# A two-block transformer kernel on one core: the gate columns of one projection last, and another order of work where the latent projections begin

## The reference, cut to what matters

```python
# first block: S = 256 rows, D = 2048, three groups of 16 heads of 128 columns
proj = rmsnorm(x, norm_b) @ w_in_b                # 3 * 2048 query columns, 2048 gate columns
q_all, gate = proj[..., :3 * D], proj[..., 3 * D:]
for g in range(3):                                # dilations 1, 4, 16
    q = apply_rope(q_all[:, :, g]); outs[g], lses[g] = dilated_window_attention(q, k, v, ...)
merged = softmax(lses over g)-weighted sum of outs
x = x + (merged * silu(gate)) @ w_out_b
# second block, where its second layer starts: x is the sum after the product with a_w_out
h_kv = rms_norm(x, kv_norm_g) * (1 + kv_scale) + kv_shift;  c_kv, k_r = split(h_kv @ kv_w_dkv)   # 576 columns
h    = rms_norm(x, norm_g[1]) * (1 + scale) + shift;        c_q, z   = split(h @ b_w_in)         # 2560 columns
```

## Time and profile before

| | |
|---|---|
| three runs | 2191.84, 2192.15, 2194.24 us; median 2192.15 |
| profiled execution | 2189.68 us, of it 2188.0 us from the first to the last instruction |
| PE busy | 2110.7 us, 96% |
| DVE, ACT busy | 1574.4 us (72%), 1097.3 us (50%) |
| mean granted clock of PE | 0.986 |
| DMA | 523.34 MB, 239 GB/s on average |

### The profile page before, as it was taken

One profiled execution on the slowest core, in us unless ns is written; L12 is line 12 of the kernel. 1 busy time (PEld: TensorE's weight loads), 2 busy tenths in 40 slices (PEclk: granted clock), 3 DMA queues, 4 the chain that ended last, 5 costly groups with the idle time before them and its releaser, 6 DMA issues.

```text
span 2188.0 us, 29739 instructions
## 1 busy us (share of the span) xinstructions
PE 2110.7 (96%) x9732; PEld 1746.1 (80%) x9732; DVE 1574.4 (72%) x2506; ACT 1097.3 (50%) x1683; POOL 11.6 (1%) x25
## 2 busy tenths in 40 slices
PE   7999999999999999979899999999999979999988
PEld 6888888888887878757788888888888868878867
DVE  5766777787879888857787778778765565556654
ACT  5444554445444444436544445454444365867742
POOL 0000000000000000000000000000000000000000
PEclk9999999999999999979999999999999989999999
DMA  7876678878766666647688777778744536433333
GB/s 294 293 281 252 239 276 320 301 283 289 264 254 235 228 256 227 222 166 259 232 296 297 289 296 298 278 293 285 301 185 173 192 125 240 173 131 139 136 134 134
DMA packets 93395, 523.34 MB, mean 239 GB/s; under 512 B 10337, under 2 KB 10593, under 8 KB 47489
## 3 DMA queue, kind: packets, MB, share of 16 engines
q1 hardware_dynamic: 90736, 509.60, 63.8%
q0 software_dynamic: 2032, 8.46, 1.1%
q10 hardware_dynamic: 544, 4.19, 0.5%
HBM read 518.01 MB, written 4.19 MB: 239 GB/s over the span
## 4 chain that ended last, share of the span: by engine, by line
PE 86%; DVE 5%; ACT 4%; issue 2%; DMA 2%; DVEq 0%; SPq 0%; ACTq 0%
PE bank L441 78%; PE bank L459 2%; DMA raw<-units 2%; DVE w_lo L1426 1%; PE bank L578 1%; ACT w_hi L847 1%; DVE ada_raw L1437 1%; PE bank L682 1%; PE bank L481 0%; PE bank L784 0%; PE bank L782 0%; PE bank L475 0%; PE bank L515 0%; DVE rbuf L1542 0%; PE bank L488 0%
## 5 line engine op out<-in xcount | busy, mean ns | idle before, releaser
L847 ACT ACTIVATE w_hi<-raw 128x1024 fp32r<-128x1024 f32 (+2 forms) x702 | 726.0, 1047 | 899.2 <-PE bank L441 665.8
L1426 DVE TENSOR_TENSOR w_lo<-raw,w_hi 128x1024 fp32r<-128x1024 f32 (+2 forms) x702 | 832.9, 1207 | 409.5 <-ACT w_hi L847 407.1
L441 PE MATMUL bank<-w_hi,xa_hi 128*128 128x512 f32 x1952 | 770.9, 395 | 5.6 <-DVE w_lo L1426 2.8
L441 PE MATMUL bank<-w_hi,xa_lo 128*128 128x512 f32 x1952 | 761.6, 390 | 0.0
L441 PE MATMUL bank<-w_lo,xa_hi 128*128 128x512 f32 x1952 | 761.2, 390 | 0.0
L441 PEld LDWEIGHTS bank<-w_hi,xa_hi 128*128 128x128 f32 x1952 | 367.7, 188 | 82.8 <-issue 6.1
L441 PEld LDWEIGHTS bank<-w_hi,xa_lo 128*128 128x128 f32 x1952 | 367.2, 188 | 77.6
L441 PEld LDWEIGHTS bank<-w_lo,xa_hi 128*128 128x128 f32 x1952 | 367.7, 188 | 74.6
L441 PE MATMUL bank<-w_hi,xb_hi 128*128 128x512 f32 (+2 forms) x864 | 336.9, 390 | 6.6 <-DVE rbuf L1563 3.6
L441 PE MATMUL bank<-w_hi,xb_lo 128*128 128x512 f32 (+2 forms) x864 | 330.2, 382 | 0.0
L441 PE MATMUL bank<-w_lo,xb_hi 128*128 128x512 f32 (+2 forms) x864 | 330.0, 382 | 0.0
(11 more groups left out here) (237 smaller groups left out, 1241.3 us busy)
## 6 DMA issues: line engine op xcount, KB each, us to landing
raw<-units SPq DMA_DIRECT2D x351, 1024.0 KB, 4.8
ada_raw<-ada_units SPq DMA_DIRECT2D x256, 512.0 KB, 5.5
rows<-ln_rows POOLq DMA_DIRECT2D x8, 512.0 KB, 3.8
res<-x SPq DMA_DIRECT2D x4, 512.0 KB, 7.6
held<-res ACTq DMA_DIRECT2D x1, 2048.0 KB, 11.9
rows<-norm_row POOLq DMA_DIRECT2D x2, 1024.0 KB, 6.2
res<-held ACTq DMA_DIRECT2D x1, 2048.0 KB, 7.8
out<-res SPq DMA_DIRECT2D x4, 512.0 KB, 7.5
```

Source lines behind the costliest of these rows:

```text
L441: last = pe.matmul(ps[t][:, 0:cols], l, r, start=c == 0 and k == 0, stop=c == CPU * units_of - 1 and k == 2)
L847: act.activation(half_of(w_hi, n0, i), half_of(raw, n0, i), ACT.Copy).then_inc(hi_done, 1)
L1426: dve.tensor_tensor(half_of(w_lo, n0, i), half_of(raw, n0, i), half_of(w_hi, n0, i), ALU.subtract)\
```

## The change

In stage in_b the order of units is now: four sets of three query blocks (12 units each, `SET_UNITS`), then four gate blocks (16 units, `GATE_UNITS`). The loops over sets are written out. A set's attention stands more densely beside the next set's units (`HEAD_STEPS`), the fourth set's beside the gate blocks; `TAIL_STEPS` is gone. `take_out` writes without the gate into `weighed` (the same storage as `gates`). ACT takes each gate block into `rbuf` (`take_gate`), DVE multiplies (`apply_gate`), and PE, ACT and DVE turn and cut the result (`turn_heads`, `split_heads`) for gate blocks 0 to 2 in the gate steps and for block 3 in out_b. Rope's pieces have new places, and a conversion can have other work between its halves (`hi_half`, `lo_half`). The 32 ada steps that in_b gives up move to out_g, and SP's loads follow.

At the border, ACT squares the first three column blocks during the second half of out_g, and the last one per tile (`add_last_out`). For each group ACT makes the dkv rows alone and copies the transposed rows to `wide` (`turned_rows`); the in_q rows are made from that copy beside dkv's second block (`late_modulated`). The eight dkv loads fetch only the 288 columns used. `turn_ahead` transposes one group a step, here and at the start of the kernel. The gains are computed earlier, halfway through out_g.

```diff
-HEAD_STEPS = {2: [("scores", 0)], 5: [("turn", 0), ("scores", 1)], 6: [("weigh", 0)],
-              8: [("turn", 1), ("scores", 2)], 9: [("weigh", 1)], 11: [("turn", 2), ("scores", 3)],
-              12: [("weigh", 2)], 13: [("turn", 3)], 14: [("weigh", 3)]}
-TAIL_STEPS = {1: [("scores", 0)], 3: [("turn", 0), ("scores", 1)], 4: [("weigh", 0)],
-              5: [("turn", 1), ("scores", 2)],
-              6: [("weigh", 1), ("turn", 2), ("scores", 3), ("weigh", 2), ("turn", 3), ("weigh", 3)]}
+HEAD_STEPS = {2: [("scores", 0)], 4: [("turn", 0), ("scores", 1)], 5: [("weigh", 0)],
+              6: [("turn", 1), ("scores", 2)], 7: [("weigh", 1)], 8: [("turn", 2), ("scores", 3)],
+              9: [("weigh", 2)], 10: [("turn", 3)], 11: [("weigh", 3)]}
...
+SET_UNITS, GATE_UNITS = 12, 16
+GATE_BLOCK0 = BLOCK0["in_b"] + 12
...
+ADA0 = {"in_a": 0, "out_a": 4, "kv": 6, "in_b": 10, "out_b": 14, "in_v": 16, "in_uz": 20, "out_g": 28}
+ADA_STEPS = [{0: 1, 1: 1, 2: 1, 3: 1, 5: 1, 7: 1, 8: 1, 11: 1}] + 3 * [{1: 2, 2: 1, 3: 1, 8: 1, 10: 1, 11: 2}] + [{}]
...
-        gates = res
+        weighed = res
...
+            n0, m0 = UNIT0["in_b"] + 4, 8 * ADA0["in_b"] + 2
+            for table in ADA_STEPS:
+                for q in range(SET_UNITS if table else GATE_UNITS):
+                    load_unit(n0)
+                    n0 += 1
+                    for _ in range(table.get(q, 0)):
+                        load_ada(m0)
...
+            while n0 < UNIT0["in_q"]:
+                sp.wait_ge(lo_done, 2 * (n0 - 2) + 2)
+                dst, src = (a.rearrange("p (i n) -> p i n", i=2)[:, :, 0:CPU // 2 * width(n0)] for a in (raw[n0 % 2][:], units[n0]))
+                sp.dma_start(dst, src).then_inc(raw_in[n0 % 2], 16)
+                n0 += 1
             with Loop(sp, (UNITS - n0) // 2) as j:
...
+                g = i + 2
+                if g < 8:
...
+            def turn_heads(b):
+                pe.wait_ge(gated, b + 1)
                 for i in range(2):
...
+            def set_step(j, q):
+                if j and q == 1:
+                    turn_q(2, j - 1)
+                for part, h in HEAD_STEPS.get(q, ()) if j else ():
+                    head_part(part, h, j - 1)
+                if j < 4 and q in (8, 11):
+                    turn_q((q - 8) // 3, j)
+                if j == 4 and q in (5, 9, 13):
+                    turn_heads((q - 5) // 4)
...
+            for j in range(4):
+                for b in range(3):
+                    product("in_b", 3 * j + b, xa, then=lambda q: set_step(j, 4 * b + q),
+                            before=None if j or b else await_rows)
...
+            def await_heads(q):
+                for i in range(2):
+                    g = g0 + 24 + 2 * q + i
+                    pe.wait_ge(turn_free[g % 2], g // 2 + 2)
+            product("out_b", 0, xb, before=await_heads, then=lambda q: turn_heads(3) if q == 0 else None)
...
+            def take_gate(b):
+                act.wait_ge(half_used, 2 * (UNIT0["in_b"] + 4 * SET_UNITS + 4 * b + 4))
+                if b:
+                    act.wait_ge(gated, b)
+                par = (GATE_BLOCK0 + b) % 2
+                for t in range(NT):
+                    act.activation(rbuf[:, t, :], banks[2 * par + t][:], ACT.Silu, scale=stat[:, 4 + t:5 + t])                        .then_inc(bank_free[par], 1)
...
+            for q in range(16):
+                if q == 0:
+                    take_gate(3)
+                elif q == 1:
+                    split_heads(3)
+                    act.wait_ge(gated, 4)
+                    act.dma_start(res[:], held).then_inc(reloaded, 16)
+                elif q == 4:
...
+                    if half == 1 and b:
+                        act.wait_ge(res_ready, 4 + b)
+                        for t in range(NT):
+                            steps.did(act.activation(ubuf[:, t, :], res[:, t, (b - 1) * NB:b * NB], ACT.Square,
+                                                     accum_out=block_sums[:, t, b - 1:b]))
...
+            for g in range(8):
+                at = TURN0["xq"] + g
+                act.wait_ge(turned, at + 1)
+                modulated(turn_bank[at % 2], g, 1, "kvshift", g)
+                act.activation(turned_rows(g), turn_bank[at % 2][:], ACT.Copy).then_inc(turn_free[at % 2], 1)
+                if g in (3, 5):
...
+            junk = [squares[:, t, :] for t in range(NT)]
+            n0 = UNIT0["dkv"] + 4
+            for q in range(4):
+                for i in range(2):
+                    late_modulated(2 * q + i)
+                split_hi(n0 + q)
+                if q == 1:
...
+            def rope_query(j, g, pieces):
+                n = 3 * j + g
+                b0 = BLOCK0["in_b"] + n
+                dve.wait_ge(half_used, 2 * (UNIT0["in_b"] + 4 * n + 4))
+                dve.wait_ge(turned, g0 + 2 * n)
+                rope([banks[2 * (b0 % 2) + t] for t in range(NT)], b0, 0, 0, pieces)
...
+            def apply_gate(b):
+                dve.wait_ge(bank_free[(GATE_BLOCK0 + b) % 2], read_out(GATE_BLOCK0 + b))
+                if b == 3:
+                    dve.wait_ge(small_free[(k0 + 79) % 2], small_read(k0 + 79))
+                for t in range(NT):
+                    last = dve.tensor_tensor(heads_out[:, t, :], weighed[:, t, b * NB:(b + 1) * NB], rbuf[:, t, :], ALU.mult)
+                last.then_inc(gated, 1)
...
+            def set_step(j, q, m):
+                n = UNIT0["in_b"] + SET_UNITS * j + q + 2
+                now, before = (HEAD_STEPS.get(i, ()) if j else () for i in (q, q - 1))
+                for part, h in now:
+                    k = k0 + 20 * (j - 1) + HEAD_USES[part, h]
                     if part == "weigh":
...
+                        take_out(h, k, j - 1)
                     elif part == "scores":
...
+                        mask_scores(k)
+                if j and q == 0:
+                    rope_query(j - 1, 2, ((0, 0), (0, S)))
+                lo_half(n, 0)
+                for part, h in now:
                     if part == "scores":
...
+                        maxima(k0 + 20 * (j - 1) + HEAD_USES[part, h])
+                for part, h in before:
+                    if part == "scores":
+                        add_groups(h, j - 1)
+                lo_half(n, 1)
+                if j and q == 0:
+                    rope_query(j - 1, 2, ((1, 0), (1, S)))
+                if j < 4 and 4 <= q < 8:
+                    rope_query(j, 0, ((q // 2 - 2, q % 2 * S),))
+                if j < 4 and q in (9, 10):
+                    rope_query(j, 1, ((q - 9, 0), (q - 9, S)))
+                if j == 4 and q in (4, 8, 12):
+                    apply_gate(q // 4 - 1)
+                if j == 4 and q in (5, 9, 13):
+                    split_heads((q - 5) // 4)
+                for i in range(ADA_STEPS[j].get(q, 0)):
+                    add_ada(m + i)
+            m0 = 8 * ADA0["in_b"]
+            for j in range(5):
...
+                if q == 1:
+                    split_heads(3)
+                if q != 15:
...
+                if q == 0:
+                    apply_gate(3)
+                if q == 7:
```

More of the change, by code:

```diff
@@ L602, in turn_heads @@
+            def turn_heads(b):
+                pe.wait_ge(gated, b + 1)
                 for i in range(2):
[L603 to L617, removed]
+                    turn(g0 + 24 + 2 * b + i, tiles(heads_out, 2 * P * i))
@@ L623, in _ @@
             for b in range(4):
[L624 to L634, removed]
@@ L637, in _ @@
[L637 to L644, removed]
+                product("in_b", 12 + b, xa, then=lambda q: set_step(4, 4 * b + q))
+            def await_heads(q):
+                for i in range(2):
+                    g = g0 + 24 + 2 * q + i
+                    pe.wait_ge(turn_free[g % 2], g // 2 + 2)
@@ L650, in turn_sum @@
                 turn(TURN0["xg"] + g, tiles(res, 2 * P * g))
-            product("out_b", 2, xb, then=turn_sum)
-            product("out_b", 3, xb, then=lambda q: turn_sum(4 + q) if q < 2 else None)
+            for b in range(1, 4):
+                product("out_b", b, xb, then=lambda q: turn_sum(2 * b - 2 + q) if q < 2 else None)
             for g in (6, 7):
@@ L1084, in _ @@
-            act.wait_ge(spilled, 16)
-            for q in range(16):
-                set_step(q, 0, False)
-                if q == 2:
-                    act.wait_ge(root_row, 1)
-                    act.activation(rows[:], rows[:], ACT.Sqrt, bias=eps).then_inc(root_row, 1)
-            with Loop(act, 3, steps) as j:
-                for q in range(16):
-                    set_step(q, j, True)
-            for q in range(6):
-                if q < 5:
-                    split_hi(UNIT0["out_b"] + q + 2)
-                if q == 0:
-                    copy_q(2, 4, 3)
-                for part, h in TAIL_STEPS.get(q, ()):
+                    copy_turned(g0 + 6 * j + 2 * g + i, side_flat[:, at:at + 2 * S])
@@ L1260, in _ @@
-            for t in range(NT):
```

(26 more changed lines are left out.)

381 lines of the change are left out of this document (182 added, 199 removed).

## The result

The changed kernel takes 2199.55 us (median of 11 runs) against 2192.15 us (11 runs): ratio 1.0035, 95% interval 1.0025 to 1.0045. It is slower by 0.35%, and the forecast was 2199.6. One of its 11 runs took 5494.45 us; the ratio leaves it out, and without it the median is 2199.3. That forecast and median agree to a tenth is partly luck: the price of the clock and the gain at the border were both too small, and they have opposite signs. The profiled execution took 2202.29 us, with a span of 2200.6 against 2188.0.

A forecast was written before the change was run, and what follows sets the result against it. PE was taken as the bound, busy 2110.7 of 2188.0 us; only its waits and clock could change. Terms 9.7 - 3.3 + 1.0 = +7.4 us on the median 2192.15 gave 2199.6 us, range 2184 to 2211.

The forecast's parts named there:

- The bank: In in_b's sets, PE waits before unit 8 for rope's last reader of the shared bank: 3.1 + 3 x 5.2 = +18.7 us.
- Rival B: At unit 8 PE does not wait, as DVE runs far enough ahead: 18.7 and its clock 7.0 fall away, 2173.9; chance 0.13.
- The third block's rope: In the next set, PE's transposes after unit 1 wait 2.5 us for rope, three times: +7.5 us.
- Block 3 of the gate: In out_b, PE's transposes behind unit 0 wait for the gate's product on DVE: +4.8 us.
- Saved in in_b: Gate columns last removes 5.3 us of waits and the tail's 25 us: -30.3 us.
- the tail: The fourth set's attention in out_b costs 25 us beyond its work, which the change removes.
- The clock: Half clock behind the idles before unit 8 and at the gate: 2.0 for each near 5 us, 1.0 for 3.1: +9.0 us.
- The border: Between out_g and in_q: rms 0.65 us earlier, groups' work shorter, DVE pacing the second dkv block: -3.3 us.
- its bound of -6: At the border, the gain if the clock rises one slow stretch earlier: -6 us.
- The forecast's bounds for a narrow load: At the border, a narrow dkv load takes 2.7 to 4.9 us, taken 3.6; at 4.9 the part gives -2.0.
- The start: Group 5's transposes come a step later, delaying unit 2's conversion and unit 4's load: +1.0 us, bounds 0 and +2.5.
- its 9.7: Part 1, gate columns last, in in_b and out_b: -30.3 + 18.7 + 7.5 + 4.8 + 9.0 = +9.7 us.

The follow-up runs named there:

- the first experiment: Changed kernel with the first query block's four rope pieces in steps 4, 5, 5 and 6 instead of 4, 5, 6 and 7: 2172.66 us, 0.9912.
- the old start: Changed kernel with the old order of the transposes in in_a alone, two groups at a time after the first two: 2198.39 us, 1.0025.
- the old border: Changed kernel with squares and root after the output product, both modulations from the turned bank, in_q behind all rows, full-width loads: 2205.74 us, 1.0060.
- the wide loads: Changed kernel with its new border, but the eight narrow units loaded at full width, 1 MB each: 2198.57 us, 1.0030.
- the second experiment: Changed kernel with the third block's rope whole before step 0's conversions, and one ada step of three sets moved from step 11 to 7: 2189.94 us, 0.9988.
- the third: Changed kernel with PE's transposes of the last gate block after out_b's unit 1 instead of unit 0, ACT's and DVE's work a step later: 2193.12 us, 1.0004.
- the two smaller moves: Third block's rope before step 0's conversions and gate block 3 one unit later; with the earlier rope piece, all on the changed kernel: 2158.41 us, 0.9845.

## Why the prediction was right, point by point

**The bank, +18.7: right.** 3.13 us once and 5.05, 5.05 and 5.06 us, 18.3 in sum. The forecast's list gave 5.8 us from unit 7's end to the last reader of the bank less 0.67 for weigh, which is 5.13 and not the 5.2 that it wrote; the chain shows 5.72 less 0.68. Rival B needed DVE to be through the piece before unit 7's end. It wasn't, and the first experiment, which puts the piece a step earlier, is rival B made true: 2172.66 us, where B said 2173.9. The Trainium skill, "TensorE: Matmul & The Clock Gate", section on architectural detail, has ACT and DVE run strictly in their order; the chain agrees: the piece starts at 631.41, at the end of the half that stands in front of it, and no earlier.

**The third block's rope, +7.5: right, with a small wait unforeseen.** 2.64, 2.15 and 2.17 us, 7.0 in sum, and three times 0.36 us at the second block's transposes, 1.1 in all.

**Block 3 of the gate, +4.8: right.** 4.75 us, through ACT's half, DVE's half, the ada step and the two products of the gate, as listed.

**Saved in in_b, -30.3: right within what can be known.** 559.45 - 546.36 = 13.1 us more. The idle measures 18.3 + 8.0 + 4.8 = 31.1, and the clock costs 13.8 (next paragraph), so what was saved is 31.1 + 13.8 - 13.1 = 31.8. The forecast's 25 for the tail is 24 by its own numbers (96.27 - 72.0 + 2.7 - 3).

**The clock, +9.0: too small.** This is the term that was mis-sized: 13.8 us. The granted clock of the changed kernel is at half in these stretches of in_b, two of them behind the third block's waits and the last behind the gate's:

```profile
549.82:553.23 3.41, 3.41 (x10) 2.67 (x9) 0.57 (x2) 0.00 (x0) 0.00 (x0) 0.50 0.95 390
631.74:635.15 3.41, 2.95 (x7) 2.40 (x8) 0.83 (x4) 0.00 (x0) 0.00 (x0) 0.50 0.73 264
676.11:679.52 3.41, 3.41 (x14) 2.92 (x13) 3.27 (x5) 1.19 (x2) 0.00 (x0) 0.50 0.51 173
723.89:730.72 6.83, 6.03 (x14) 4.82 (x15) 1.17 (x5) 0.00 (x0) 0.00 (x0) 0.50 0.42 154
816.05:819.46 3.41, 2.94 (x7) 2.36 (x8) 0.84 (x4) 0.00 (x0) 0.00 (x0) 0.50 0.76 257
860.43:863.84 3.41, 3.41 (x11) 2.73 (x10) 1.40 (x2) 1.06 (x2) 0.00 (x0) 0.50 0.46 137
962.83:969.66 6.83, 5.48 (x17) 4.71 (x18) 2.81 (x8) 1.32 (x4) 0.00 (x0) 0.50 0.90 314
```

PE works for 27.6 us in them, of which half, 13.8, is lost: 7.7 behind the four idles before unit 8 (forecast 7.0), 2.7 behind the gate's (forecast 2.0), and 3.4 behind the third block's waits. These last are most of the error: the forecast put them at nothing, because the clock held around 2.32 us.

How much is lost changes from one execution to the next. Three experiments leave the code of in_b as it is (the old start, the old border, the wide loads). They have the same waits to 0.5 us, in_b takes 557.24, 558.41 and 558.23 us in them, and the loss counted in the same way over the whole of in_b is 11.8, 13.1 and 13.2 us, against 13.9 here. So a difference between two single windows of in_b is uncertain by some 2 us. Within that the experiments agree: filling the four idles shortens in_b by 9.0, taking them out by 24.65, 6.3 more than the idle; the second experiment shortens it by 10.7 for 6.9 of idle, the third by 6.0 for 3.6. By the ratios the four idles' share is 10.5 and 8.7.

The timeline of PE in the changed kernel shows the third block's three waits (in square brackets):

```profile
675.81 1.72 PE L490 MATMUL bank<-tab,rbuf 128*128 128x128 f32 x8 [2.64 <-DVE rbuf L1587]
...
769.26 1.09 PE L490 MATMUL bank<-tab,rbuf 128*128 128x128 f32 x8 [2.15 <-DVE rbuf L1587]
...
859.62 1.24 PE L490 MATMUL bank<-tab,rbuf 128*128 128x128 f32 x8 [2.17 <-DVE rbuf L1587]
```

The eight transposes take 1.09 us at full clock. Behind 2.64 and behind 2.17 they take 1.72 and 1.24, since the clock goes down to half during them, and behind 2.15 nothing happens. In the three other traces the first wait, 2.41, 2.37 and 2.17 us, is not followed by half clock either, and the last, 2.16 and 2.17, is each time.

**The border, -3.3: right in mechanism, too small.** The windows say -5.3, undoing it costs 5.5. Of the 5.3, 1.18 are the earlier rms (forecast 0.65) and 4.15 lie between the transposes and in_q (forecast 2.6). The clock has a part in this that the forecast's sum left out and its bound of -6 named: half clock comes in two stretches before and in one after.

```profile
1773.68:1787.34 13.66, 7.30 (x31) 6.92 (x32) 9.36 (x17) 9.67 (x22) 0.00 (x0) 0.50 0.12 49
1794.16:1797.58 3.42, 3.23 (x14) 3.23 (x15) 3.35 (x7) 2.71 (x7) 0.00 (x0) 0.50 0.15 17
...
1788.85:1799.09 10.24, 6.02 (x26) 5.63 (x27) 6.26 (x11) 6.37 (x16) 0.00 (x0) 0.50 0.19 59
```

PE works for 10.5 us in the first two and for 6.0 in the third, so about 2.3 of the 5.3 us are clock; PE's idle in the window, 50.07 - 35.60 = 14.5 before and 44.73 - 33.11 = 11.6 after, is the rest. Units of the second block follow each other in 3.46 us, where 3.7 were forecast for DVE's pace, and no load holds them up. The forecast's bounds for a narrow load decided nothing: with loads of 1 MB the time is the same. The profile's page gives 4.1 us from issue to landing for the narrow loads, of which it counts six of 576 KB and not eight, and 4.9 for the wide ones; the 3.6 taken was too low. The estimate of 3.4 by the Trainium skill, "DMA: Bandwidth & Descriptors", section on the anatomy of one DMA, is lower still; the measurement, 4.1, decides, and the skill's figure was for the POOL path.

**The start, +1.0: not settled,** 0 to 2 us.

**The sum.** In the profiled execution in_b gives +13.1, the border -5.3, the start +2.2 and the stage behind the border 371.19 - 368.51 = +2.7: 12.6 in all. The last two are no work of the change as far as can be seen. The stage behind the border takes 370.1 to 371.5 us in all ten kernels that follow the kernel before here, also in the one with the old border, with PE idle as long as before (20.5 against 20.6 us). The difference is clock: PE works for 14.0 us at half clock there in the changed kernel's trace and for 8.3 before, 2.9 us more lost; why it was granted so stays open. On the medians the difference is 7.4 us: 13.1 - 5.3 = 7.8 with nothing for the start, or 5.6 with the shortest in_b of the four traces. The forecast had 9.7 - 3.3 + 1.0. In_b cost 3.4 more than its 9.7 (clock 4.8 and idle 0.1 more, saving 1.5 more), the border gave 2.0 more, the start cost 1.0 less if it cost nothing, and these nearly cancelled.

## What to carry to other kernels

When a loop is cut to an odd number of blocks over a pair of banks, list what stands in front of the bank's last reader on its engine at the moment when the next block wants the bank. Here one piece of rope behind one conversion cost 27 us, more than the change could win at the tail. Moving it by a step made the change faster than the kernel before (0.9912), and with the two smaller moves it is worth 1.5%. Price an idle of PE with its own length and the clock behind it: by the granted clock the idles of 3 to 5 us before unit 8 cost 1.4 times their length in all, (18.3 + 7.7) / 18.3.

## What was not expected

- Useless transposes in a wait made the kernel 10.5 us faster: idles of 18.3 us in sum, filled down to 1.9, gave back 10.5 us although the product behind them started no sooner after unit 7.
- Idles of 2.17 and 2.15 us had different consequences: half clock behind the one, full clock behind the other. An idle's length alone does not say it.
- Loads of 576 KB land in 4.1 us, those of 1 MB in 4.9, and at this border it makes no difference.
- Up to in_b's first unit, the eight kernels with the same code differ by as much as 4.2 us (497.63 to 501.84). A term of 1 us at the start can't be read from one trace.
